# The seam between the context stage and the first layer: stores on their own semaphore, earlier taps, clear, row fetches and softmaxes

## The reference, cut to what matters

```python
def first_block(x, ...):            # 2 layers
    for l in range(DEPTH):
        mix = hybrid_mixer(x, w_in[l], conv_w[l], w_out[l], rel_bias)   # retention, attention, convolution
        x = layer_norm(DN_ALPHA * x + mix, ln1_g[l], ln1_b[l])
        f = conv_ffn(x, w_up[l], ffn_conv_w[l], w_down[l])
        x = layer_norm(DN_ALPHA * x + f, ln2_g[l], ln2_b[l])
    return x

def second_block(x, c, ctx, c_ctx, w_mod, b_mod, ...):    # 2 layers
    for l in range(DEPTH):
        sh1, s1, g1, sh2, s2, g2 = jnp.split((sc @ w_mod[l] + b_mod[l]), 6)        # modulation rows of the latent stream
        csh1, cs1, cg1, csh2, cs2, cg2 = jnp.split(sc_ctx @ w_mod[l] + b_mod[l], 6)      # and of the context stream
        # context stream (layer 0: whole; layer 1: its keys and values only), latent stream,
        # attention of the latent stream over both, convolution branch, and in each:
        x = x + g2 * peer(modulate(x, sh2, s2), ...)
        if not last:
            h_ctx = h_ctx + cg2 * peer(modulate(h_ctx, csh2, cs2), ...)

def peer(h, w_pq, sub_keys, u_tab, v_tab):
    # 128 picks (8 heads x 16) of 16384 experts for each token
    w = jax.nn.softmax(best_s, axis=-1)
    u = jnp.take(u_tab, ec, axis=0)                            # gathered rows
    act = jax.nn.gelu(jnp.einsum('cd,ced->ce', hc, u), approximate=False)
    v = jnp.take(v_tab, ec, axis=0)
    return jnp.einsum('ce,ced->cd', (act * wc), v)
```

## Time and profile before

| | us |
|---|---|
| median of 3 runs | 2988.73 |
| lowest, highest | 2986.16, 2989.93 |
| profiled execution, span | 2956.6 |
| median less that span | 32.1 |

### The profile page before, as it was taken

How to read it: one execution, slowest core, us unless ns; L and a number is a source line. 1 busy time by engine, 2 the same in 40 slices (tenths; PEclk the granted TensorE clock), 3 DMA queues, 4 the chain that set the end, 5 groups by cost and what they waited for, 6 DMA issues and landing times.

```text
span 2956.6 us, 27829 instructions
## 1 busy us (share of the span) xinstructions
PE 2457.2 (83%) x8610; PEld 1390.2 (47%) x8610; DVE 2104.7 (71%) x4478; ACT 819.5 (28%) x2274; POOL 1124.3 (38%) x1121
## 2 busy tenths in 40 slices
PE   6995897987897989888799787778897897877776
PEld 4664464765556566565444333323374443333322
DVE  1659479788888978787777677754376776777654
ACT  1231111000012000023444333334324443443443
POOL 1100444766554666470233333333211333333332
PEclk9988887998996999999999899899998998999999
DMA  8348999999999999980799999999732998999998
GB/s 348 147 182 346 368 415 362 379 410 412 408 396 362 404 410 413 383 299 1 284 399 410 368 420 416 414 411 386 322 117 101 363 416 359 420 418 419 414 420 336
DMA packets 183478, 1038.89 MB, mean 351 GB/s; under 512 B 26971, under 2 KB 28978, under 8 KB 99876
## 3 DMA queue, kind: packets, MB, share of 16 engines
q0 software_dynamic: 147456, 805.37, 67.6%
q1 hardware_dynamic: 35292, 230.38, 19.5%
q10 hardware_dynamic: 584, 1.36, 0.1%
HBM read 1032.60 MB, written 4.44 MB: 351 GB/s over the span
## 4 chain that ended last, share of the span: by engine, by line
DMA 32%; PE 27%; DVE 26%; issue 7%; POOL 4%; ACT 4%; SPq 0%; ACTq 0%; DVEq 0%; POOLq 0%
DMA W<-in_peer_uv,IDX 14%; PE PS L2693 13%; PE PS L333 9%; DMA ROWS<-in_peer_uv,IDX 8%; DMA ROWS<-in_peer_uv,COEF 3%; DVE ROWS L1341 3%; DVE ROWS L2316 3%; POOL ROWS L2524 3%; DVE W L2829 2%; DMA ROWS<-in_peer_uv,IDXV 2%; DVE PROD L2329 1%; DMA G<-in_peer_uv,IDX 1%; PE PS L2127 1%; PE PS L469 1%; PE PS L2117 1%
## 5 line engine op out<-in xcount | busy, mean ns | idle before, releaser
L2693 PE MATMUL PS<-W,SCALE 128*128 128x512 f32 x1712 | 840.5, 638 | 219.6 <-ACT SCALE L2777 219.5
L2829 DVE CUSTOM_DVE_ANT_0 W<-W,PS 128x1024 f32<-128x1024 f32 x428 | 515.2, 1219 | 336.4 <-DMA W<-in_peer_uv,IDX 335.0
L2882 POOL DMA_INDIRECT W<-in_peer_uv,IDX x428 | 408.0, 953 | 684.6 <-PE PS L2693 667.0
L2693 PEld LDWEIGHTS PS<-W,SCALE 128*128 128x128 f32 x1712 | 332.0, 203 | 707.9 <-issue 706.4
L2524 POOL DMA_INDIRECT ROWS<-in_peer_uv,IDX x206 | 219.8, 1067 | 401.1 <-DVE IDX L1638 150.3
L2117 PE MATMUL PS<-XT,W 128*128 128x256 f32 x1408 | 307.2, 379 | 0.0
L2117 PEld LDWEIGHTS PS<-XT,W 128*128 128x128 f32 x1408 | 267.7, 190 | 45.5 <-issue 10.1
L2770 ACT ACTIVATE DOT<-DOT 128x1 f32<-128x1 f32 x512 | 103.6, 202 | 651.5 <-DVE DOT L2829 644.2
L333 PE MATMUL PS<-W,XT 128*128 128x512 f32 (+2 forms) x576 | 222.1, 548 | 10.8 <-ACT XT L948 5.7
L333 PE MATMUL PS<-XT,W 128*128 128x128 f32 (+1 forms) x1344 | 218.2, 323 | 3.7 <-ACT XT L1061 3.7
L2777 ACT ACTIVATE SCALE<-C,COEF 128x128 f32<-128x128 f32 x512 | 205.6, 402 | 49.4 <-PE PS L2693 2.7
(11 more groups left out here) (407 smaller groups left out, 3127.4 us busy)
## 6 DMA issues: line engine op xcount, KB each, us to landing
W<-in_w_up SPq DMA_DIRECT2D x44, 1024.0 KB, 12.1
W<-in_w_in SPq DMA_DIRECT2D x21, 2048.0 KB, 11.1
W<-in_w_mod SPq DMA_DIRECT2D x7, 4096.0 KB, 12.7
W<-in_w_down SPq DMA_DIRECT2D x22, 1024.0 KB, 8.0
W<-in_peer_wq SPq DMA_DIRECT2D x6, 2048.0 KB, 9.1
W<-in_w_o SPq DMA_DIRECT2D x6, 2048.0 KB, 9.6
W<-in_w_out SPq DMA_DIRECT2D x4, 2048.0 KB, 11.7
W<-in_peer_uv,IDX POOLq DMA_INDIRECT x428, 12.7
```

The costliest lines, as they stand in the source:

```text
L2693: ins = nc.tensor.matmul(PS[:, SUMS2[t] + h, :], SCALE[:, n % NSCALE, :], v_of(n)[:, h * 512:(h + 1) * 512], start=m == 0, stop=m == PICKS ...
L2829: nc.vector.tensor_tensor_reduce(u_of(n), u_of(n), h_of(t), 1.0, 0.0, ALU.mult, ALU.add, DOT[:, t, m:m + 1]).then_inc(s.rows_used, 1)
L2882: nc.gpsimd.indirect_dma_start(pair_slot(n), None, in_pairs, bass.IndirectOffsetOnAxis(IDX[:, t, m:m + 1], 0),).then_inc(pair_landed[fetch ...
```

## The change

The first block's start is rearranged; nothing that is computed changes.

- The two stores of the bias tables count on a semaphore of their own (`bias_stored`). SP waits for it ahead of the loads of `DEC` and `G`; POOL waits for it ahead of row 6 (rows 6 and 7 lie where the tables lay).
- `raw_load(sp, 0)` stands in the set-up, at the start of the program, behind the loads of the second block's first four weight chunks.
- POOL clears layer 0's semaphores when `mod 9` is done and read (`mod_read` 10), and fetches rows 2 to 9 when the second tile's picks are there, no more behind `mod 11`.
- TensorE, in `bias_pe`, waits until ScalarE has read all six tables.
- ScalarE runs the two softmaxes ahead of its part of `mod 10`, and copies `H` to PSUM ahead of its part of `mod 11`. It still waits for the stores of `mod 11` before it copies the turned `x`.
- TensorE waits for `mod_read` 12 where the clear behind `mod 11` stood; `x` counts on `ctx_loaded`, whose second increment it is.
- VectorE does 6 dot products, then copies the taps' columns, then the other 36.
- `SC` moves from `DOT` (which the dot products write) to a free part of `G`.

```diff
-        x_loaded = sem("x_loaded")
+        bias_stored = sem("bias_stored")
...
-        SC = DOT[:].rearrange("p t n -> p (t n)").rearrange("p (k m) -> p k m", k=DK)
+        SC = G[:, SC_AT:SC_AT + DK * 32].rearrange("p (k m) -> p k m", k=DK)
@@ bias_pe @@
+                pe.wait_ge(s.score_read, MOBA_H)
+                banks.read_out.clear()
@@ bias_act @@
-                act.dma_start(bias_dram[:, 0:5 * NB], AR[:, 6 * D:6 * D + 5 * NB]).then_inc(s.stored, 16)
-                act.dma_start(bias_dram[:, 5 * NB:6 * NB], HANK[5]).then_inc(s.stored, 16)
+                act.dma_start(bias_dram[:, 0:5 * NB], AR[:, 6 * D:6 * D + 5 * NB]).then_inc(bias_stored, 16)
+                act.dma_start(bias_dram[:, 5 * NB:6 * NB], HANK[5]).then_inc(bias_stored, 16)
@@ setup_sp @@
                 for c in range(WS):
                     first_load(sp, c, L)
+                raw_load(sp, 0)
@@ context_sp @@
-                sp.dma_start(X[:], x_dram).then_inc(x_loaded, 16)
+                sp.dma_start(X[:], x_dram).then_inc(ctx_loaded, 16)
...
-                sp.wait_ge(layers[0].stored, 3 * 16)
-                raw_load(sp, 0)
                 sp.wait_ge(s.groups_done, groups.of("mod", 11))
@@ context_act @@
                 for g in range(MOD_BESIDE, L * MODS_N):
+                    if g == L * MODS_N - 2:
+                        for t in range(TT):
+                            softmax_act(act, s, BC, t, 0, EH, 1 + t + 1)
+                    if g == L * MODS_N - 1:
+                        act.wait_ge(cleared, 1)
+                        first_h_in_psum(act, 0)
                     mod_act(act, s, groups, g)
                     if g == BIAS_BEHIND:
                         bias_act(act)
-                for t in range(TT):
-                    softmax_act(act, s, BC, t, 0, EH, 1 + t + 1)
                 mod_stored_to(act, L * MODS_N - 1)
@@ first_pe @@
                         pe.wait_ge(cleared, 1)
                         pe.wait_ge(layers[1].act_out_ready, 1 + TT)
                         pe.wait_ge(layers[1].weights_spread, TT)
-                        pe.wait_ge(x_loaded, 16)
+                        pe.wait_ge(mod_read, L * MODS_N)
+                        pe.wait_ge(ctx_loaded, 2 * 16)
@@ first_sp @@
+                        sp.wait_ge(bias_stored, 2 * 16)
                         sp.dma_start(DEC[:].rearrange("p h n -> p (h n)"), A["decay"]).then_inc(tables_loaded, 16)
@@ first_dve @@
-                        columns(l)
...
-                    dots(EARLY, in_psum)
+                    if l == 0:
+                        dots(BEFORE_COLUMNS, in_psum)       # 6
+                        columns(l)
+                    dots(EARLY - taken["dots"], in_psum)
@@ first_pool @@
                         if l == 0 and n == 2:
                             pool.wait_ge(raw_loaded, 16 * 2)
-                            pool.wait_ge(layers[1].groups_done, of_context.of("mod", L * MODS_N - 1))
+                            pool.wait_ge(layers[1].groups_done, of_context.of("mod", 9))
+                            pool.wait_ge(mod_read, 10)
                             clear_layer(pool, 0)
                         if l == 0 and n in (0, 2):
                             pool.wait_ge(layers[1].picks_ready, 1 + n // 2)
-                        if l == 0 and n == RING:
-                            pool.wait_ge(layers[1].groups_done, of_context.of("mod", 9))
+                        if l == 0 and n == 6:
+                            pool.wait_ge(bias_stored, 2 * 16)
```

More of the change, by code:

```diff
@@ L96 @@
 LEFT = 26
+SC_AT = 2 * HD + P + 3 * CW2
 LEFT_FIRST, LEFT_SECOND = 5, 8
@@ L1871, in context_sp, with first_h_in_psum @@
                 mod_stored_to(sp, 11)
+            def first_h_in_psum(act, l):
+                nc.scalar.copy(PS[:, 6:8, :].rearrange("p n d -> p (n d)"), H[:, l, :]).then_inc(layers[l].h_copied, 1)
             def context_act(act):
@@ L1968, in program @@
             EARLY, TURNED, PER_HEAD, LATE = 42, 6, 2, 24
+            BEFORE_COLUMNS = 6
             DOTS = [8, 12, 12]
@@ L2226, in h_in_psum @@
                         act.wait_ge(layers[l - 1].down_read, 2 * TT)
-                    nc.scalar.copy(PS[:, 6:8, :].rearrange("p n d -> p (n d)"), H[:, l, :]).then_inc(layers[l].h_copied, 1)
+                    first_h_in_psum(act, l)
                 for l in range(L):
@@ L2233, in first_act @@
                         act.wait_ge(layers[1].weights_spread, TT)
-                        h_in_psum(l)
                         x_turned(l, 0)
```

## The result

The changed kernel took 2993.07 us (median of 20 runs, 2983.20 to 3000.90), the kernel before 2985.44 us beside it (20 runs, 2977.36 to 2991.60). The ratio is 1.0025, with a 95% interval of 1.0015 to 1.0035: 7.6 us slower, where 2.3 us faster was forecast.

What follows compares the result with a forecast made beforehand. TensorE's start was taken to decide when the heads begin, with VectorE carrying them. The terms, 0.15 (x copy) + 0 (clock) + 2.14 (row waits) = 2.3 us, took the median from 2988.73 to 2986.4 us; range 2981.5 to 2990.0.

Steps and rivals of the forecast that it cites:

- What bounds the kernel, and that TensorE's start sets the heads: Context stage to heads: TensorE's start decides when the heads begin, VectorE carries them; 7.2 us of transfer time unused.
- The hole fills, the clear and the taps leave the path: 296.6 to 304.6 us: early rows, 4.2 MB, fill the idle DMA time; clear and row fetches no longer wait for group 11.
- Not at 313: Sign behind group 11: TensorE turns RAW at about 313, with no release by POOL.
- Step 1: Group 10 to group 11: bias row takes 3.0 us (bounds 1.5, 4.6), group 11 5.9; group 11 ends 2.0 later.
- Step 2: ScalarE's wait before the x copy: group 11's stores land in 5.0 us (bounds 1.5, 6.6); x gains 0.15 us.
- The heads' row waits go, 2.14 us: In the heads, VectorE's waits for rows of 1.47 and 0.67 us at 431.33 and 433.23 disappear.
- The wait ahead of row 6: POOL's new wait for the bias stores costs nothing: they must be done by row 6's turn at about 300.5.
- Clock 0: First two projections: no gain counted from TensorE's granted clock, bounds 0 and 2.8 us; about 4 us idle stay ahead.
- The 32.1 us around the span: Whole kernel: the same 32.1 us added around the forecast span of 2954.3 us to give the median.
- Rival 2: Small transfers between group 10 and the x copy both at the slow end: 1.2 us slower, 2989.9 us; 15%.
- Rival 3: First projections: gathers starve TensorE of w_in's chunk 2, 7.9 us slower, 2996.6 us; 5%.
- Rival 4: Heads: early rows make no odds, VectorE's two row waits stay; 0.15 us gained, 2988.6 us; 10%.

Runs made afterwards that it cites:

- plain loads: Rows behind group 11, columns first, plus eight plain 512 KB loads by SyncE in the gathers' former place; 2966.55 and 2995.14 us, 1.0026 and 1.0018 of the kernel before.
- the second run: The changed kernel run again, nothing altered; 2993.84 us against 2985.13 for the kernel before, ratio 1.0029.
- both edits: Changed kernel, with group 11's bias row loaded with group 10's and ScalarE's store wait behind its first two x copies; 0.9989 and 0.9974 of the kernel before.
- the second trace of before: The kernel before run once more, nothing altered; 2958.24 us against 2960.27, ratio 0.9993.

## Why the prediction was wrong

- *What bounds the kernel, and that TensorE's start sets the heads*: right, though the start came later and not sooner. 9.98 us at the heads for 10.95 at the first projection.
- *The hole fills, the clear and the taps leave the path*: right; `RAW` is turned at 322.54, at once behind ScalarE's read of group 11, with no release by POOL. Not at 313, because of what follows.
- *The failed step is Step 1, "two small transfers in series"*: it counted the transfers on the path and took TensorE's own part as fixed ("SP issues group 11's bias row when group 10 is done, at 303.4"; "Group 11 itself takes 5.35, or 6.08"). Measured: the signal came at 308.97, 5.6 us late on that account, and group 11 took from 312.97 to ScalarE's store at 322.06, 9.1 instead of 6.9. The bias row itself took 4.0, inside the bounds of 1.5 and 4.6, 1.0 above the value taken. No term and no rival had TensorE, or its signal, held up by gathers. The runs show that it comes with more than four rows fetched early, in the series at 2985 us and above, and that plain loads at this place don't bring it; by what way stays open.
- *Step 2, the stores' landing*: mis-sized. The prediction took 5.0 us with a bound of 6.6; it was 7.7 from the second store's issue (322.57) to the x copy (330.27). 5.0 lay below both loaded cases that it had itself, 5.9 and 6.6, and the bound was read from group 4's stores, at another place. Beside w_in alone the stores took 5.9, so 0.9 of the error has nothing to do with rows. The step adds 2.7 us: 5.6 + 1.0 + 2.2 + 2.7 = 11.5, the difference between the forecast x copy (318.8) and the real one (330.27).
- *The heads' row waits go, 2.14 us*: right, 2.3 in the trace. The wait ahead of row 6, put at nothing, was 1.0 us on POOL (2.2 in the second run), off the path.
- *Clock 0*: close. The first two projections took 15.55 against 16.52, 1.0 us back.
- *The 32.1 us around the span*: misread. In the runs of after time and span differ by 2.1 us (2988.41, 2986.3). The trace of before was of a shorter execution, like those of the series at 2960 us. The sum wasn't harmed, since it stood on differences.
- *Rival 2, slow small transfers*, had the right direction, but its price was too low: 3.3 us at the x copy, where 11.3 came (330.27 against 318.95), and 1.2 us in all, where 7.6 came. Rival 3 didn't occur: the projections have no gaps from weights. Rival 4 is refuted with the heads' waits.

The Trainium skill (DMA: Bandwidth & Descriptors, Latency and other measured facts) says that memory access is slower under high load, 2 us instead of 0.2, and that this dominates a transfer's fixed cost; here 512 KB gathers and 2 MB chunks were in flight beside a store of 4 KB, and its landing of 7.7 us is well above that, so the page alone would have mis-sized it too.

Open: by what way gathers hold up TensorE or its signals; why only in some series; and what the changed kernel itself takes in a series at 2960 us (it wasn't run there; that kernels with eight early rows and both edits were 0.1 to 0.3% faster than before there suggests that it loses less).

## What to carry to other kernels

Before filling idle transfer time, list what small transfers and signals the next stage needs in series, and take them out of the way first (load the row one step earlier, wait for stores only where their source is overwritten); then fill with no more than fits, here four of eight rows (eight did no harm in the series at 2960 us, and cost 6 to 12 us in the others). A copy that frees a bank for TensorE doesn't belong behind work that waits for gathers. And take a second trace of the kernel before if its span doesn't fit its times: a difference of 32 us between a span and a median is a sign of an unusual execution, not a cost around it.

## What was not expected of the hardware

In all traces from the series at 2985 us and above, and in none from those at 2960, TensorE issues some 40 of the second layer's instructions (products and weight loads) one by one, 0.7 to 1.4 us apart, with no releaser. The changed kernel's second run, then the kernel before from a series at 2960 us:

```profile
861.06 0.59 PE L334 MATMUL PS<-W,XT 128*128 128x512 f32 x1 [2.21 <-issue]
863.16 1.01 PE L334 MATMUL PS<-W,XT 128*128 128x512 f32 x1 [1.51 <-issue]
...
880.07 1.01 PE L334 MATMUL PS<-W,XT 128*128 128x512 f32 x1 [1.08 <-issue]
```

```profile
833.44 42.36 PE L333 MATMUL PS<-W,XT 128*128 128x512 f32 x122
```

It begins at the same instructions whatever the time (within 15 of the 6700th of TensorE's), while gathers fill the engines. From the 6600th to the 6800th of TensorE's records it is 42.1 to 42.5 us in the seven traces without it (one of them is the trace of before that the prediction read) and 62.7 to 68.1 in the thirteen with it: 20 to 26 us, most of the 25 to 31 between the series. That the kernel before has it too in those series is inferred from its times, not seen. Each of the five series of experiments ran on another chip (numbers 13, 5 and 8 where before takes 2985 us or more, 15 and 10 where it takes 2960), so the condition may lie in the chip; since none came up twice, that isn't shown. In the traces without the stretch gathers fill the engines at this place too (68.6% of their time in the second trace of before, 834 to 876 us), so full engines alone don't bring it. The queues in that stretch of the changed kernel's second run (860 to 888 us):

```profile
q0 software_dynamic: 2525, 9.18, 82.1%
q1 hardware_dynamic: 217, 2.24, 19.0%
q14 instruction: 1, 0.01, 0.1%
```

The late signals of groups 10 and 11 look alike (gaps without releaser, gathers in flight, the same series), but that both have one cause is argued, not shown. The Trainium skill (Runtime: NRT & Kernel Launch, Instruction fetch mechanics) says that an engine's instructions come in blocks of 16 KB, the next one while the one before runs, mostly hidden. The trace shows just one instruction packet in these 28 us, and no wait that names one; if this is a late supply of instructions, it isn't hidden here, and no run tells.
